# Two latent norms in one PSUM bank, stacked compressed values, and a reordered run-up to attention

## The reference

```python
def rms_norm(x, g):
    y = xf * lax.rsqrt(jnp.mean(xf * xf, axis=-1, keepdims=True) + EPS)
    return (y * g.astype(jnp.float32)).astype(x.dtype)
q  = (rms_norm(cq, q_norm) @ w_uq)      # cq: 512 x 256
kv = (rms_norm(ckv, kv_norm) @ w_ukv)   # ckv: 512 x 128
```

```python
p_cmp = masked_softmax(s_cmp, cmp_mask)          # heads x 512 x 31
o_cmp = jnp.einsum('bgrsn,bgnd->bgrsd', p_cmp, vc)
o = g[0] * o_cmp + g[1] * o_slc + g[2] * o_win
```

## Time and profile before

| | us |
|---|---|
| median of 3 runs | 1513.03 (1512.39 to 1513.38) |
| the profiled execution, whole | 1513.47 |
| its span, first to last instruction | 1511.7 |
| PE (matmul) busy | 1491.4 (99%) |
| DVE, ACT, POOL busy | 890.4, 716.1, 438.6 |
| mean granted TensorE clock, as a share of full speed | 0.999 |

### The profile page before, as it was taken

The page is one execution under the profiler, slowest core; times in us unless marked ns, Lnnn a source line. Parts: engine busy times, 40 slices in busy tenths (PEclk is TensorE's granted clock), DMA queues, the critical chain, the costliest instruction groups (busy, mean ns, idle before and its releaser), DMA issues.

```text
span 1511.7 us, 21055 instructions
## 1 busy us (share of the span) xinstructions
PE 1491.4 (99%) x7300; PEld 1248.2 (83%) x7300; DVE 890.4 (59%) x1539; ACT 716.1 (47%) x1308; POOL 438.6 (29%) x459
## 2 busy tenths in 40 slices
PE   8999999999999999999999999999999999999998
PEld 6888888887888888888888888888888888888886
DVE  6876766767553544535557776667575535354453
ACT  6864777873431222222367557888544222122222
POOL 1302667773020101101022046778711101010111
PEclk9999999999999999999999999999999999999999
DMA  5344221135233333322323522212432333223323
GB/s 212 98 142 145 70 85 64 56 99 181 86 96 98 98 98 97 97 97 97 98 84 126 172 82 68 78 50 78 133 125 84 98 98 98 97 97 97 97 98 112
DMA packets 43362, 154.29 MB, mean 102 GB/s; under 512 B 5440, under 2 KB 5440, under 8 KB 43280
## 3 DMA queue, kind: packets, MB, share of 16 engines
q1 hardware_dynamic: 37296, 133.77, 27.5%
q0 software_dynamic: 5696, 18.94, 3.5%
q10 hardware_dynamic: 288, 0.52, 0.1%
HBM read 142.73 MB, written 10.49 MB: 101 GB/s over the span
## 4 chain that ended last, share of the span: by engine, by line
PE 86%; DVE 4%; ACT 4%; issue 3%; DMA 1%; POOL 0%; POOLq 0%; DVEq 0%; SPq 0%; ACTq 0%
PE G L1518 14%; PE G L1520 13%; PE G L1519 13%; PE O L1520 9%; PE O L1519 9%; PE O L1518 9%; PE O L1811 3%; PE T L1787 3%; PE T L1518 2%; PE T L1520 2%; PE T L1519 2%; PE S L1762 2%; ACT F L697 1%; PE O L1593 1%; PE S L1768 1%
## 5 line engine op out<-in xcount | busy, mean ns | idle before, releaser
L645 ACT ACTIVATE wsplit<-stage 128x1024 fp32r<-128x1024 f32 x227 | 240.2, 1058 | 598.7 <-PE G L1520 272.6
L1012 DVE TENSOR_TENSOR wsplit<-stage,wsplit 128x1024 fp32r<-128x1024 f32 x180 | 262.8, 1460 | 72.8 <-ACT wsplit L645 72.5
L631 POOL TENSOR_TENSOR F<-Y 128x512 f32<-128x512 f32 x64 | 68.5, 1070 | 637.2 <-DVE Y L1476 637.2
L1518 PE MATMUL G<-xg,wsplit 128*128 128x512 f32 x560 | 223.6, 399 | 7.3 <-DVE wsplit L1038 7.1
L1519 PE MATMUL G<-xg,wsplit 128*128 128x512 f32 x560 | 219.7, 392 | 0.0
L1520 PE MATMUL G<-xg,wsplit 128*128 128x512 f32 x560 | 219.4, 392 | 0.0
L529 POOL TENSOR_TENSOR wsplit<-stage,wsplit 128x1024 fp32r<-128x1024 f32 x46 | 112.0, 2434 | 126.0 <-ACT wsplit L645 125.5
L1249 DVE CUSTOM_DVE_ANT_0 F<-S,F 128x512 f32<-128x512 f32 (+3 forms) x176 | 89.0, 506 | 90.5 <-PE S L1762 61.6
L816 ACT ACTIVATE F<-F,nmx 128x512 f32<-128x512 f32 (+3 forms) x176 | 101.4, 576 | 66.8 <-DVE nmx L1249 64.9
L1518 PEld LDWEIGHTS G<-xg,wsplit 128*128 128x128 f32 x560 | 105.8, 189 | 28.9 <-DVE wsplit L1038 7.1
L1518 PE MATMUL G<-area,wsplit 128*128 128x512 f32 x320 | 124.7, 390 | 0.3
(11 more groups left out here) (300 smaller groups left out, 3045.6 us busy)
## 6 DMA issues: line engine op xcount, KB each, us to landing
stage<-units SPq DMA_DIRECT2D x229, 512.0 KB, 3.5
stage_n<-units_n SPq DMA_DIRECT2D x20, 512.0 KB, 3.6
gates<-Y POOLq DMA_DIRECT2D x32, 256.0 KB, 3.0
E<-gates POOLq DMA_DIRECT2D x24, 256.0 KB, 3.1
F<-gates POOLq DMA_DIRECT2D x8, 256.0 KB, 4.1
x<-x_in SPq DMA_DIRECT2D x3, 512.0 KB, 6.5
rope<-tables POOLq DMA_DIRECT2D x1, 768.0 KB, 6.4
out<-F SPq DMA_DIRECT2D x3, 256.0 KB, 2.3
```

The costliest lines, as they stand in the source:

```text
L631: pool.tensor_tensor(F[:, m % 2, :], Y[:, m % 2, :], Y[:, m % 2, :], ALU.mult)\
L645: act.activation(wslot(u)[:, 0, :], staged(u), ACT.Copy).then_inc(s_whin if u in SN else s_whi, 1)
L1012: dve.tensor_tensor(wslot(u)[:, 1, :], staged(u), wslot(u)[:, 0, :], ALU.subtract)\
L1518: pe.matmul(dst, a(0), b(0), start=first, stop=False)
```

## The change

1. Norms. `halves` is a new constant, 64 columns of 0.5, 64 of 0 and 64 of 1. The squares stay 128x512; ScalarE writes their rounded part (`c_squares_hi`, at Q2) and GpSimd the remainder. After MISC four fp32r products, with [0.5 | 0] and with [0 | 1], fill one bank: partitions 0 to 63 hold the query sum, 64 to 127 the key/value sum, already spread. ScalarE takes one root over 128x512 (`c_root`, at MISC), VectorE one reciprocal over 128x512 (`c_inverse`, at GATE0), and ScalarE copies the halves to all partitions by three 64x512 copies (`c_factors`, at GATE1, ahead of the tanh of GATE1 and of the narrow split for W1.6). `c_norm` moves to GATE2, W1.6 and W1.7. `c_mean_squares`, `c_diagonals` and the two fp32 spreads go.
2. Stacked values. Hi and lo of `pcT` stand one above the other in the partitions, so that one product per head remains of two. Each split of WT is now two instructions of 64x512 on ScalarE and two on VectorE.
3. Later turns. WT0 and WT1 move from steps 10 and 12, ahead of the gate piece, to steps 11 and 13, behind it.
4. Queue order. On ScalarE and VectorE the split of CQ1 moves from CQ0 to Q0, ahead of `swap` and `rotated` of Q0; that of W1.1 from CQ1 to Q1; `blocks(1)` on VectorE from KW to V1, behind the split of CQ0.

```diff
-SMALL_AT = {("CQ", 1): [1], ("CQ", 2): [2], ...
+SMALL_AT = {("CQ", 2): [2], ...
-FILL[10].append((("WT", 0), 0))
-FILL[12].append((("WT", 1), 0))
...
+FILL[11].append((("WT", 0), 0))
+FILL[13].append((("WT", 1), 0))
...
+            for n, value in enumerate((0.5, 0.0, 1.0)):
+                pool.memset(halves[:, 64 * n:64 * n + 64].bitcast(F32), value).then_inc(s_halves, 1)
...
+                pool.wait_ge(s_csqhi, l + 1)
+                pool.tensor_tensor(CSQ[:, 0:4:2, :], csq[:, 0:3:2, :], CSQ[:, 1:4:2, :], ALU.subtract).then_inc(s_csqlo, 1)
...
+                def c_squares_hi():
+                    act.activation(CSQ[:, 1:4:2, :], csq[:, 0:3:2, :], ACT.Copy).then_inc(s_csqhi, 1)
                 def c_root():
+                    act.wait_ge(s_cspread, l + 1)
+                    act.activation(csq[:, 0, :], g_tile(("CB", 0))[:, :], ACT.Sqrt, scale=1.0 / 128, bias=eps)
+                def c_factors():
+                    act.wait_ge(s_cinv, l + 1)
+                    act.activation(csq[0:64, 2, :], csq[64:128, 0, :], ACT.Copy)
+                    act.activation(csq[64:128, 2, :], csq[64:128, 0, :], ACT.Copy).then_inc(s_cfactor, 1)
+                    act.wait_ge(s_cfactor, l * 2 + 1)
+                    act.activation(csq[64:128, 0, :], csq[0:64, 0, :], ACT.Copy).then_inc(s_cfactor, 1)
...
+                    if item == ("GATE", 1):
+                        c_factors()
...
+                def c_inverse():
+                    dve.wait_ge(s_croot, l + 1)
+                    dve.reciprocal(csq[:, 0, :], csq[:, 0, :]).then_inc(s_cinv, 1)
...
                 def compressed_hi(gr):
-                    act.activation(pcT[:, gr, 0, :], g_tile(("WT", gr))[:, :], ACT.Copy).then_inc(s_cThi, 1)
+                    for two in range(2):
+                        ins = act.activation(pcT[0:64, gr, two, :], g_tile(("WT", gr))[64 * two:64 * two + 64, :], ACT.Copy)
...
+                def c_spread():
+                    for kind in range(2):
+                        for c in range(2):
+                            ins = pe.matmul(g_tile(("CB", 0))[:, :], halves[:, 64 * kind:64 * kind + P], CSQ[:, 2 * kind + 1 - c, :],
+                                            start=kind == 0 and c == 0, stop=kind == 1 and c == 1)
...
-                        for c in range(2):
-                            pe.matmul(dst[:, :], vblk[:, gr, b, :], pcT[:, gr, c, :], start=False, stop=False,
+                        pe.matmul(dst[:, :], vblk[:, gr, b % 2, :], pcT[:, gr, b // 2, :], start=False, stop=False,
```

More of the change, by code:

```diff
@@ L56 @@
 BN.update({NU + b: NB + b for b in range(2)})
-SMALL_AT = {("CQ", 1): [1], ("CQ", 2): [2], ("Q", 2): [3], ("MISC", 0): [4], ("Q", 3): [5],
+SMALL_AT = {("CQ", 2): [2], ("Q", 2): [3], ("MISC", 0): [4], ("Q", 3): [5],
             ("GATE", 1): [7], ("GATE", 2): [8], ("GATE", 3): [9]}
@@ L753, in c_square @@
                     act.activation(csq[:, c, :], E[:, c, :], ACT.Square).then_inc(s_csq, 1)
+                def c_squares_hi():
+                    act.wait_ge(s_csq, l * 3 + 3)
+                    act.wait_ge(s_csum, l + 1)
+                    act.activation(CSQ[:, 1:4:2, :], csq[:, 0:3:2, :], ACT.Copy).then_inc(s_csqhi, 1)
                 def c_root():
[L756 to L760, removed]
+                    act.wait_ge(s_cspread, l + 1)
+                    act.activation(csq[:, 0, :], g_tile(("CB", 0))[:, :], ACT.Sqrt, scale=1.0 / 128, bias=eps)\
+                        .then_inc(s_croot, 1)
+                def c_factors():
[4 more added lines that the diff above has]
+                    act.activation(csq[64:128, 0, :], csq[0:64, 0, :], ACT.Copy).then_inc(s_cfactor, 1)
                 def c_hi(c):
@@ L793, in vc_hi @@
                         src = g_tile(("W2V", 0))[rows, 0:2 * HD].rearrange("p (g n) -> p g n", g=2)
-                        ins = act.activation(vblk[rows, :, b, 0:HD], src, ACT.Copy)
+                        ins = act.activation(vblk[rows, :, b % 2, 0:HD], src, ACT.Copy)
                     ins.then_inc(s_kchi, 1)
@@ L910, in _ @@
                         hidden_tanh(0)
+                    if item == ("Q", 0):
+                        split_hi(l, BIG[BN[u + 1] + 2])
+                    if item == ("Q", 1):
+                        split_hi(l, SMALL[1])
                     if item in ROPED and ROPED.index(item) > 2:
@@ L1139, in nsa_gates @@
                     dve.tensor_scalar(gt[:, :, :], gt[:, :, :], 0.5, 0.5, ALU.mult, ALU.add).then_inc(s_gfree, 1)
[L1141 to L1150, removed]
+                def c_inverse():
+                    dve.wait_ge(s_croot, l + 1)
+                    dve.reciprocal(csq[:, 0, :], csq[:, 0, :]).then_inc(s_cinv, 1)
                 def c_norm(c):
-                    dve.wait_ge(s_cspread, l * 2 + (c // 2 + 1))
+                    dve.wait_ge(s_cfactor, l * 2 + 2)
                     gain = par[:, PR_QN + c:PR_QN + c + 1]
-                    dve.scalar_tensor_tensor(E[:, c, :], E[:, c, :], gain, g_tile(("CB", c // 2))[:, :],
+                    dve.scalar_tensor_tensor(E[:, c, :], E[:, c, :], gain, csq[:, c // 2 * 2, :],
                                              ALU.mult, ALU.mult).then_inc(s_cf, 1)
-                    if c > 0:
-                        dve.wait_ge(s_cf, l * 3 + (c + 1))
-                        dve.sem_inc(s_gfree, 1)
                 def c_lo(c):
@@ L1241, in compressed_lo @@
                     dve.wait_ge(s_cThi, l * 2 + (gr + 1))
-                    dve.tensor_tensor(pcT[:, gr, 1, :], g_tile(("WT", gr))[:, :], pcT[:, gr, 0, :], ALU.subtract)\
-                        .then_inc(s_gfree, 1)
+                    for two in range(2):
+                        ins = dve.tensor_tensor(pcT[64:128, gr, two, :], g_tile(("WT", gr))[64 * two:64 * two + 64, :],
+                                                pcT[0:64, gr, two, :], ALU.subtract)
+                    ins.then_inc(s_gfree, 1)
                 def max_of(i):
@@ L1360, in _ @@
                         evac(item, item, Y[:, i % 2, :])
-                    if 0 < u and u in BN and item != ("GATE", FIRST_GATE - 1) and name not in ("VC", "KS", "V", "KW"):
+                    if 0 < u and u in BN and item not in (("GATE", FIRST_GATE - 1), ("CQ", 0)) and name not in ("VC", "KS", "V", "KW"):
                         split_lo(l, BIG[BN[u] + 2])
@@ L1384, in _ @@
                         key_sum()
-                        for c in range(3):
-                            c_norm(c)
+                        dve.wait_ge(s_croot, l + 1)
+                        dve.sem_inc(s_gfree, 2)
                     if item == ("Q", 3):
@@ L1390, in _ @@
                         hidden(0)
+                    if item == ("Q", 0):
+                        split_lo(l, BIG[BN[u + 1] + 2])
+                    if item == ("Q", 1):
+                        split_lo(l, SMALL[1])
                     if item in ROPED and name not in ("KS", "KW"):
@@ L1395, in _ @@
                         q_lo(3)
+                        c_inverse()
+                    if item == ("GATE", 2):
+                        c_norm(0)
+                    if item == ("W1", 6):
+                        c_norm(1)
+                    if item == ("W1", 7):
+                        c_norm(2)
                     if item == ("W1", 7):
@@ L1650, in weights_T @@
                     ins.then_inc(s_cT, 1)
[L1652 to L1668 removed]
+                def c_spread():
+                    free(("CB", 0))
+                    pe.wait_ge(s_halves, 3)
+                    pe.wait_ge(s_csqlo, l + 1)
+                    for kind in range(2):
+                        for c in range(2):
+                            ins = pe.matmul(g_tile(("CB", 0))[:, :], halves[:, 64 * kind:64 * kind + P], CSQ[:, 2 * kind + 1 - c, :],
+                                            start=kind == 0 and c == 0, stop=kind == 1 and c == 1)
+                    ins.then_inc(s_cspread, 1)
                 def gate(i, piece):
```

48 lines of the change are left out of this document (17 added, 31 removed).

## The result

The changed kernel takes 1516.07 us (median of 18 runs, 1514.70 to 1516.92), the kernel before 1513.12 in the same sessions (18 runs, 1512.39 to 1513.93): ratio 1.0018, 95% interval 1.0011 to 1.0024. It is 2.9 us slower, where 1507.3 was forecast and 1511.9 was the upper end of the range. The difference is just under the 0.2% within which the prediction called a result no change; with 18 runs on either side it is still no accident. The profiled execution of the kernel after took 1514.7 us (span 1512.9), as fast as any of the 18 and 1.4 us under the median. It was lucky, and why is part of the answer.

A forecast was written before the change was run, and what follows sets the result against it. TensorE's queue was taken to set the end almost everywhere. The terms summed to 2.90 us gained per layer, 5.8 for two, taking the profiled 1513.47 to 1507.7, or 1507.3 as median; range 1501.8 to 1511.9.

The forecast's parts named there:

- splits: Pauses ahead of CQ0, CQ1 and W1.1 go, gaining 1.83 us per layer; 0.2 charged for splits that become late.
- stacked values: Compressed values in attention: one of two products goes for eight heads, saving 1.84 us per layer.
- norms, inverse, around MISC: Per layer: norm products save 2.68 us; pauses after MISC cost 0.15 and 0.3, the one at W1.6 2.6.
- turns: WT0 and WT1 turned later: net cost 0.2 us per layer, bounds gain 0.5 and cost 1.0.
- the inverse: VectorE's 128x512 reciprocal at GATE0 takes 3.6 us, bounds 0.68 and 8.1.
- the relay through ScalarE: After the reciprocal, ScalarE's copies, tanh and narrow rounding, then VectorE's remainder for W1.6, all move by 4.35 us.
- the pause: TensorE waits 2.5 us ahead of W1.6, plus 0.1 of restart: 2.6 us per layer.
- rival D: The pause lets TensorE's clock drop, 2.5 us per layer more: 1512.4 us, no change; chance 6%.
- E: The wide inverse makes the kernel slower: at 4.7 us, W1.6 pauses 3.7 and the clock drops, 1514.5 us; chance 5%.
- The bounds: Charge for splits late after reordering, 0 to 1.6 us per layer; at worst Q1 late by 0.7, CQ2 by 0.9.
- rival C: The three early pauses only move on, Q1 and CQ2 wait instead; 3.7 us lost, 1511.0 us; chance 11%.
- The sign that I named for having them too cheap: A long wait of O's first product at step 15 would show the turns were priced too low.

The follow-up runs named there:

- run 6: Kernel before with only the earlier splits of CQ1, W1.0 and W1.1 and blocks(1) moved to V1: 1510.75 us.
- run 1: Kernel before with the stacked compressed values alone, norms, splits and turns as before: 1513.53 us.
- run 2: Kernel before with the stacked values and the new norms, splits and turns as before: 1517.97 us.
- run 5: Kernel after with nine unread products of 512 columns on TensorE ahead of W1.6's wait: 1512.26 us.
- run 3: Kernel after with the turns of the compressed weights back at steps 10 and 12: 1515.61 us.
- run 8: run 7 with the rounding of the other branch's compressed queries and keys put off to steps 18 to 20 and 19 to 21: 1507.35 us.
- run 9: Kernel before with only the rounding of the other branch's compressed queries and keys put off: 1513.11 us.
- run 10: Kernel before with stacked values, VectorE starting after each stacked copy, and the other branch's rounding put off; old norms, splits and turns: 1512.08 us.
- run 11: run 8 with the first queries' difference on VectorE one item later, behind the splits of CQ2 and W1.1: 1506.80 us.
- run 4: Kernel after with the turns back at steps 10 and 12 and the wide inverse moved from GATE0 to GATE3: 1508.88 us.
- run 7: run 4 with VectorE starting on the first 64 stacked rows once ScalarE has copied them: 1508.79 us.

## Why the prediction was wrong

Differences of medians, both layers, in us; a minus is faster.

| part | forecast | measured | by |
|---|---|---|---|
| splits | 2 x (-1.83 + 0.2) = -3.3 | -2.4 | run 6 |
| stacked values | 2 x -1.84 = -3.7 | +0.4 | run 1 |
| norms, inverse, around MISC | 2 x (-2.68 + 0.15 + 0.3 + 2.6) = +0.7 | +4.4, of it 3.2 to 3.8 the clock | runs 2, 5 |
| turns | 2 x 0.2 = +0.4 | +0.5 | run 3 |
| sum | -5.8 | +2.9 | after: +2.9 |

The parts add up, though the third row is good to about 2 us only, and the +0.4 and +0.5 can't be told from no change. Of the miss of 8.8 us, 4.1 lie in the stacked values, 3.7 in the norms' row, 0.9 in the splits and 0.1 in the turns.

**One step that failed is the clock.** The sum put it at nothing; it cost 1.6 us a time and, by the estimate above, came twice in most executions. The forecast had the inverse (taken 3.6, measured 3.35), its place, the relay through ScalarE and the pause (taken 2.6, measured 2.54) right, and the reason for rival D too, and gave it 6%. I argued that no pause of 2.5 us was in the trace and that those under 1 us cost nothing. That is a gap in the evidence, not evidence; the only long idle in the trace, the one at the start, had been followed by the half clock. E, which carried the same drop to "slower", I made depend on an inverse of over 4 us. The drop needed no such thing. (Its 1514.5 was also inside the 0.2% that I had called no change, so by my own bound it was not "slower".) The size of a drop was below D's: 1.6 us a time by the starts, where I had taken 2.5 from the kernel's start. D alone, at 1512.4, would have been too fast as well: no rival had the clock and the stacked values fail together.

**The other, as large, is the stacked values.** Forecast -3.7, measured +0.4. "Neighbouring starts leave no gap that could swallow it" is true of where the products are and not of where their operands are made. The prediction even wrote that a split of 2 + 2 instructions on 64 partitions takes twice as long as one on 128, and charged that to the turns only, at WT1's end. It missed the step between: WT1's transposes share WT0's bank, so with the turns two steps apart at 10 and 12 the doubled copy and difference of WT0 stand ahead of them. That costs 1.3 us per layer, and 1.2 instead of 1.84 is saved behind it. Runs 8 to 10 show that the queues around it were a part: putting off six instructions that cost nothing in the kernel before (run 9) gave 1.4 us in run 8.

**The splits** went the way they were worked out: CQ0, CQ1 and W1.1 start without idle. CQ2, given 0.1 us of cover, is late: the timeline of PE after
```profile
67.85 0.50 PE L1547 MATMUL G<-xg,wsplit 128*128 128x512 f32 x1 [0.45 <-DVE wsplit L1039]
```
shows 0.45 and its restart, and about 0.3 in the second layer. The bounds had it at up to 0.9; rival C, where the other items wait too, did not come. The remainder of CQ2 itself was not stretched (1.22 us, from 66.58); two operations ahead of it on VectorE were, 1.60 in place of 0.69 at 60.68 and 1.72 in place of 1.22 at 62.80, both beside GpSimd's work on the keys (56.42 to 63.43). (In the kernel before that work ran from 42.24 to 49.79, beside the long remainder of CQ0; the earlier trace rows does not show it.) Run 11 shows that another order on VectorE is enough to remove the pause.

**The norms on TensorE and around MISC** hold: 0.99 for the four products against 0.92; the transposes at 88.62 wait 0.15, 0.4 in all by their starts against 0.3.

**The turns** were forecast at 0.4 and measured at 0.5, which can't be told from no change: the term is neither confirmed nor refuted. The sign that I named for having them too cheap, a long wait ahead of the second head's first values, did appear (1.24 us, answering to the earlier trace rows). Timeline of PE after:
```profile
170.41 0.39 PE L1549 MATMUL G<-xg,wsplit 128*128 128x512 f32 x1
172.05 0.41 PE L1828 MATMUL O<-area_b,area 128*128 128x128 f32 x2 [1.24 <-DVE pcT L1260]
```
It misled: run 3 shows that without the late turns about the same time is lost earlier, ahead of WT1's transposes. A wait names who came last, not which edit is to blame.

**One loss I read and did not test.** In the profiled execution the kernel after leads by 1.3 us at the end of the first layer's attention (335.40 for the last values, 336.70 before) and by 0.1 at 368. Timeline of GpSimd and VectorE at the layer's merge, then that of PE:
```profile
346.03 2.39 POOL L534 TENSOR_TENSOR wsplit<-stage,wsplit 128x1024 fp32r<-128x1024 f32 x1 [0.56 <-ACT wsplit L652]
...
346.35 2.62 DVE L1488 TENSOR_TENSOR F<-F,E 128x512 f32<-128x512 f32 x1
```
```profile
353.83 0.39 PE L1549 MATMUL S<-xg,wsplit 128*128 128x512 f32 x1
355.24 0.50 PE L1547 MATMUL T<-xg,wsplit 128*128 128x512 f32 x1 [1.02 <-POOL wsplit L534]
```
An addition that takes 0.69 us elsewhere takes 2.62 here, where it starts 0.3 us behind a split of GpSimd; ScalarE's queue and GpSimd's next split move back with it, and TensorE waits 1.02. In the kernel before the same addition started 0.4 us ahead of that split and took 0.69. The Trainium skill (SBUF — State Buffer, "Who interferes with whom") says that a VectorE instruction with two SBUF inputs and a GpSimd instruction that reads SBUF exclude each other. The trace agrees: the addition ends at 348.97, 0.55 behind GpSimd's split at 348.42. In run 5, whose first layer differs only by the filled pause and by its start, the addition starts 0.6 us ahead of the split and no such loss occurs. Of the other profiled executions only run 11's has it (2.71 us for the addition, a wait of 1.04). So the relative timing of two queues looks like the cause, and not an edit; no run tests this.

## What to carry to other kernels

Price a pause of TensorE twice: by its length, and by the half clock that may follow. One of 2.4 us cost 1.6 us more here, in one layer or both of an execution; where the wait can't be removed, products that nobody reads may pay for themselves. When products are saved by preparing their operands in another shape, follow the preparation through its bank and its queues; here a doubled copy, with the queues around it, ate the whole saving. A long instruction such as a wide reciprocal belongs where its engine is idle, not where its result is first ready: moved by three gate units, at unchanged length, it turned +2.9 into -4.2 us together with the turns.

## What the runs showed of the hardware

- VectorE's reciprocal of 128x512 takes 3.35 us, 6.5 ns per column, near the 6.3 that the narrow ones give; the Trainium skill (VectorE: DVE Perf Modes, the walkthrough of the 8-slice pipeline) gives a repeat count of 8, from which I had estimated 4.4 (eight cycles per column alone make 4.3). The measurement decides.
- After 2.38 us without a product the granted clock was 0.50 for about 3 us in some layers and 1.00 in others of one and the same kernel: second layer only (after, run 2), first only (run 3). It was down by the first product behind the pause in run 3 and fell 1.5 us after that product in the kernel after.
- The half clock also came where no pause near it was over 0.2 us. Near the kernel's end TensorE makes many narrow products (128x128, and 128x1 with 0.16 us of idle ahead). In the profiled execution of run 9, whose products there are those of the kernel before, the granted clock was 0.50 in this stretch, and the kernel before had 1.00 (views of run 9, then of before):
```profile
1502.00:1504.00 2.00, 2.00 (x12) 0.50 0.18 70
1502.00:1504.00 2.00, 2.00 (x21) 1.00 0.04 8
```
- At the start of the kernel, too, the number of products at half speed changes from one execution to the next: 12 before, 6 after, 8 in runs 3, 4 and 5, 14 in runs 6 and 7, and 6 in run 9, whose program differs from before only in the attention. At 0.2 us each the eight between 6 and 14 are 1.6 us of luck between two profiles, which is why terms here are taken from medians.
- Copies of 64 partitions on ScalarE took 0.59 to 0.63 each, differences on VectorE 0.70: as long as those of 128.
